# The value sums of the decode sequences in two accumulator banks by turns

## The chip, the cores and the metric

One core of one Trainium2 chip runs the whole program in one launch. The metric is the device time in microseconds (us). The kernel before takes 1522.09 us, the median of 3 runs (1521.27 to 1523.09).

## What is computed

One inference step of a decoder layer. 1024 prompt tokens go through a projection, causal differential attention (4 heads), a diagonal state-space mixer ("S5"), an output projection and a routed mixture of experts. Eight further sequences, of one new token each, go through the same layer, but their attention reads a paged cache of 8192 past positions: 64 pages of 128 positions for keys and as many for values, 256 KB a page and cache. For each of these sequences the reference has

```
s = einsum(q, k_all);  p = softmax(s)
a = p[:, :, 0] - lam * p[:, :, 1]
o = einsum('bhqk,bkhe->bqhe', a, v_all)
o = o * rsqrt(mean(o * o)) * subln_g * (1 - lambda_init)
```

The change is in the sums over `v_all` of these eight sequences.

## The kernel before, in words

**Passes.** The eight sequences are taken in two passes x of four (`SPP` = 4). A pass has a key part (units `K`), its softmax (`m1`, `m2`, `m3`, `pt`), and then the four sequences y = 0 to 3 of the value part, one after the other. The pages of a sequence come in eight steps `V(x, y, t, g)` of eight pages: t is the quarter (0 to 3), g the half of the ring of 16 page buffers that the step reads. Each step is two parts p of four pages. TensorE multiplies a page with a block of the transposed weights `sall` and adds into the PSUM bank `SC`, all eight steps of a sequence into the same sums; behind the last part stands one product for the new token (`dv`, `ptn`), which signals `s_pv`. Then comes `ov(b)`, b = 4x + y: VectorE copies the 128x512 sums to `o4s` (L1181), scales a small map (L1182) and signals `s_o4`; TensorE multiplies `o4s` with the map, four "closing" products into `aP`, four columns of the bank `OD`; VectorE copies these to `aD` (L1185). In the trace every matmul has the line L1756; a value step shows as SC<-ring,sall x16, the new token as SC<-dv,ptn, the closing products as OD<-wmap,o4s.

**Waits.** There is one bank for the sums, so the first step of the next sequence waits for the copy: `pe.wait_ge(s_o4, SPP * x + y)` (L1934). The pages are loaded by SyncE (L484); it waits before each four of them until TensorE is done with the buffers (`s_pgfree`). A TensorE step waits until its four pages are there (`landed`).

**The order.** Nothing is reordered at run time. `streams()` writes ten lists of units, each with an assumed cost and what it must come after; `make_plan()` (L177) merges them into one list, at each step the first list (`dec`, with K, V and ov) that is ready. Value steps become ready by assumed page landings and a fixed pace, so their place depends little on the other units. Every engine then runs its own share of each unit in this one order, and an engine that waits in one unit does nothing of a later one. Units on the way:

- prompt side: `q` projection and its rotation on VectorE, `qt`, and for each of 8 row blocks and 4 heads `S` (scores, VectorE takes the maximum), `C` (VectorE combines the two softmaxes), `T` (transposes), `O` (product with V), `AN` and `ot` per block;
- S5: `bA`, `bP`, `bK`, `bX`, `bH` (the scan, a long VectorE unit), `bY`, `bG`, `bS`, in four rounds;
- the end: `out` (output projection), `hn`, `hs`, `hT`, `r` (router), then the routing chain `pick1`, `pick2`, `rank`, `rt0`, `rt1`, `ids`, `lists`. `lists` (L1628, VectorE) has a part that needs nothing of `ids` and one that does, and ends in the signal `s_route` (L1663), for which the first expert weights (SyncE, L503) and the first gather of rows (GpSimd, L671) wait. `dout`, `dout2` and `out(8)` finish the eight sequences.

Around each change of sequence the order of the kernel before is:

- 0 to 1: V(0,0,3,1), bG(2,1), q(0,0), bS(2), bU(3), bA(3), q(0,1), V(0,1,0,0), ov(0), bP(3), V(0,1,0,1), qt(0)
- 1 to 2: C(0,3), bX, q(3,0), V(0,1,3,1), C(1,0), T(0,3), bH(3), q(3,1), V(0,2,0,0), ov(1), O(0,3), T(1,0), S(1,1), AN(0), V(0,2,0,1), C(1,1), ot(0)
- 2 to 3: V(0,2,3,1), O(2,1), S(2,2), V(0,3,0,0), ov(2), S(2,3)
- after 3: V(0,3,3,1), C(4,0), T(3,3), q(6,1), ov(3), O(3,3), K(1,0,0,0)
- 4 to 5: V(1,0,3,1), hs(2), out(3,1,0), hT(2), V(1,1,0,0), ov(4), r(2)
- 5 to 6: V(1,1,3,1), r(4), out(5,1,1), V(1,2,0,0), ov(5)
- 6 to 7: V(1,2,3,1), hn(7), hs(7), V(1,3,0,0), ov(6), hT(7), r(7), V(1,3,0,1), pick1
- after 7: rt1, V(1,3,3,0), ids, V(1,3,3,1), lists, ov(7), dout, dout2, out(8), turn0

Behind the plan stands the mixture of experts, a loop over experts whose weights (3 MB each) are loaded four ahead.

Of the kernel before, what the change touches and what calls it, by code (L numbers as in the profile page):

```python
# [6 lines left out]
SEQ, NB, D = 1024, 8, 1024  # L7
# [9 lines left out]
GRP = 8  # L17
TURNS = NPAGE // RING
SPP = 4
# [60 lines left out]
def streams():  # L80

    dec = []
    for x in range(NPASS):
        for t in range(TURNS):
            for g in range(2):
                for y in range(SPP):
                    dec.append((("K", x, t, g, y), 1.95, [(("ov", SPP * x - 1), 0.8)] if x else []))
        dec += [(("m1", x), 0.8, [(dec[-1][0], 0.9)]), (("m2", x), 0.3, [(("m1", x), 3.3)]),
                (("m3", x), 0.3, [(("m2", x), 1.0)]), (("pt", x), 2.3, [(("m3", x), 3.2)])]
        for y in range(SPP):  # L90
            b = SPP * x + y
            for t in range(TURNS):
                for g in range(2):
                    late = [(("pt", x), 1.2)] if t + g + y == 0 else [(dec[-2][0], 1.2)] if t + g == 0 else []
                    dec.append((("V", x, y, t, g), 1.95, late))
                    if t + g == 0 and y:
                        dec[-1], dec[-2] = dec[-2], dec[-1]
            dec.append((("ov", b), 0.4, [(("V", x, y, TURNS - 1, 1), 1.5)]))
    dec += [(("dout",), 0.1, [(("ov", NB - 1), 1.0)]), (("dout2",), 0.2, [(("dout",), 2.0)]),
            (("out", NT), 4.0, [(("dout2",), 1.0), (("out", NT - 1, 1, 1), 0.0)]), (("hn", NT), 0.0, [(("out", NT), 2.0)]),  # L100
            (("hs", NT), 0.0, [(("hn", NT), 2.5)]), (("hT", NT), 1.0, [(("hs", NT), 0.8)]),
# [146 lines left out]
def hymba_step(nc, io):  # L248
# [13 lines left out]
    with ctx:  # L262
# [122 lines left out]

        SC = ctx.enter_context(nc.psum_tensor("SC", [128, 512], f32))
        OD = ctx.enter_context(nc.psum_tensor("OD", [128, 512], f32))
        nkP, mxT, mbP, lP, aP = OD[0:32, 0:NB], OD[0:1, 128:256], OD[:, 256:257], OD[:, 257:258], OD[:, 260:264]
        WA = ctx.enter_context(nc.psum_tensor("WA", [128, 512 * BANKS], f32))
        W = [WA[:, 1024 * i:1024 * i + 1024] for i in range(3)]  # L390

# [580 lines left out]
        def _(dve):  # L972
# [196 lines left out]
            def pt(x):  # L1169
                dve.wait_ge(s_pexp, x + 1)  # L1170
                dve.tensor_tensor(mrow[:, 2:3], mrow[:, 2:3], mrow[:, 3:4], ADD)
                dve.drain().then_inc(s_l, 1)

            def ov(b):
                x, y = divmod(b, SPP)
                if y == 0:
                    dve.wait_ge(s_lP, x + 1)
                    dve.reciprocal(mrow[:, 4:5], lP)
                    dve.drain()
                dve.wait_ge(s_pv, b + 1)  # L1180
                dve.tensor_copy(o4s[:, :], SC[:, :])  # L1181
                dve.tensor_scalar(wmap[:, SPP, :], wmap[:, y, :], mrow[:, 4:5], None, MUL)  # L1182
                dve.drain().then_inc(s_o4, 1)  # L1183
                dve.wait_ge(s_aP, b + 1)
                dve.tensor_copy(aD[:, :, b], aP)  # L1185
                dve.drain().then_inc(s_ad, 1)

            def dout():
# [483 lines left out]
            def turn0():  # L1672
# [1 line left out]
                dve.drain().then_inc(free_sem("t0"), 1)  # L1674

            todo = {"stats": stats, "dqkv": dqkv, "dprep": dprep, "u": u, "k": k, "q": q, "S": S, "C": C, "O": O, "AN": AN,
                    "m1": m1, "m2": m2, "m3": m3, "pt": pt, "ov": ov, "dout": dout, "dout2": dout2, "s5a": s5a, "bA": bA, "bK": bK,
                    "bE": bE, "bH": bH, "bY": bY, "bG": bG, "glu": glu, "out": out_, "hn": hn, "hs": hs, "hT": hT,
                    "r": r_, "pick1": pick1, "pick2": pick2, "rt0": rt0, "rt1": rt1, "lists": lists, "turn0": turn0}
            for unit in PLAN:  # L1680
# [73 lines left out]
        def _(pe):  # L1754
# [163 lines left out]
            def pt(x):  # L1918
                pe.wait_ge(s_pexp, x + 1)
                for n in range(4):  # L1920
                    vacant(pe, "PT", x, n)
                    for j in range(4):
                        last = pe.transpose(slot("PT", x, n)[:, 128 * j:128 * j + 128],
                                            sall[:, n, 128 * j:128 * j + 128], ident)
                    last.then_inc(full_sem("PT", x, n), 1)
                vacant(pe, "PTn", x)
                pe.transpose(slot("PTn", x)[0:NB, 0:128], snew[:, :], ident).then_inc(full_sem("PTn", x), 1)
                pe.wait_ge(s_l, x + 1)
                mm(lP, consts[:, C_SUM:C_SUM + 128], mrow[:, 2:3]).then_inc(s_lP, 1)

            def Vv(x, y, r, g, p):
                if r + g + p == 0:
                    if y:
                        pe.wait_ge(s_o4, SPP * x + y)  # L1934
                    else:
                        pe.wait_ge(s_ptw, x + 1)
                landed(x, SPP * UPB + UPB * y + 2 * r + g, g, p)
                for j in range(p, GRP, PARTS):

                    t, q, c = j // 2, j % 2, j // 2  # L1940
                    blk = sall[:, r, 256 * g + 128 * q:256 * g + 128 * q + 128]
                    last = mm(SC[32 * c:32 * c + 32, :], blk[:, 32 * t:32 * t + 32], ring[:, GRP * g + j, :],
                              r + g + p == 0, r == TURNS - 1 and g == 1 and p == PARTS - 1 and c > 0,
                              skip_group_check=True)
                last.then_inc(s_pgfree, 1)
                if r == TURNS - 1 and g == 1 and p == PARTS - 1:
                    mm(SC[0:32, :], ptn[:, 0:32], dv[:, :], False, True, skip_group_check=True).then_inc(s_pv, 1)

            def ov(b):
                pe.wait_ge(s_o4, b + 1)  # L1950
                for h in range(H):
                    last = mm(aP[:, h:h + 1], o4s[:, 128 * h:128 * h + 128], wmap[:, SPP, h:h + 1])
                last.then_inc(s_aP, 1)

            def dout():
# [325 lines left out]
```

## Time and profile before

| what | value |
|---|---|
| median of 3 runs | 1522.09 us |
| the profiled execution | 1525.98 us |
| its span, first to last instruction | 1524.3 us |
| TensorE busy | 1307.3 us, 86% of the span |
| VectorE busy | 522.8 us, 34% |
| ScalarE, GpSimd busy | 247.9, 212.9 us |
| DMA | 458.35 MB, mean 301 GB/s |
| mean granted TensorE clock | 0.923 of full speed |

The page also has the span in 40 slices of 38 us. The first pass of value sums lies between 325 and 587 us, the second between 838 and 1069 us, the experts from about 1086 to 1470 us. In a timeline row the bracket at the end is the idle time of that engine before the row and what ended it. The granted clock has two levels, 1.0 (2.4 GHz) and 0.5 (1.2 GHz); a figure between is a mean over a stretch.

### The profile page before, as it was taken

Reading aid. Unit: us, or ns where it says so; the run is one execution under the profiler, and the core shown is the slowest. Engines: PE = TensorE matmul, PEld = TensorE weight load, DVE = VectorE, ACT = ScalarE, POOL = GpSimd, SP = SyncE. Lnnn points to the kernel's source line nnn. Section 1 sums busy time; section 2 is a strip of 40 time slices with the busy share of each in tenths; the row PEclk is TensorE's granted clock in tenths of the full one; section 3 lists DMA queues with packets and bytes.
Section 4 is the critical chain, followed back from the end, with each engine's and each line's share of the span. In section 5 each row is a group of like instructions: output and inputs, shape, how many; then the busy total and the mean of one; then the engine's idle time right before and its main releaser. Section 6 shows DMA issues by size and latency. Waiting matters only on the chain.

```text
span 1524.3 us, 26488 instructions
## 1 busy us (share of the span) xinstructions
PE 1307.3 (86%) x8952; PEld 686.1 (45%) x8952; DVE 522.8 (34%) x1430; ACT 247.9 (16%) x473; POOL 212.9 (14%) x327
## 2 busy tenths in 40 slices
PE   4899899999878877999877999986789999999930
PEld 2455565654424334666663434343344444444410
DVE  1452334443375354554431111134221211111227
ACT  2100111121112122332321000000011111111111
POOL 1102104041300200000010000000122222222111
PEclk9899999999898889999899999986899999999975
DMA  9499989889788976898897979897979999999854
GB/s 356 172 322 297 318 271 305 317 249 324 244 274 273 334 274 233 313 344 312 275 325 287 330 248 336 293 317 254 359 278 356 366 368 364 360 351 357 299 180 195
DMA packets 186454, 458.35 MB, mean 301 GB/s; under 512 B 24177, under 2 KB 24561, under 8 KB 177778
## 3 DMA queue, kind: packets, MB, share of 16 engines
q1 hardware_dynamic: 165906, 394.41, 73.6%
q0 software_dynamic: 20448, 62.59, 12.6%
q8 instruction: 66, 1.08, 0.3%
q14 instruction: 34, 0.28, 0.1%
HBM read 421.92 MB, written 33.80 MB: 299 GB/s over the span
## 4 chain that ended last, share of the span: by engine, by line
PE 67%; DMA 11%; DVE 9%; SPq 4%; issue 4%; DVEq 2%; ACT 1%; POOL 1%; ACTq 0%; POOLq 0%; PEldq 0%
PE WA L1756 48%; PE SC L1756 10%; PE OD L1756 4%; DMA ring<-in_cacheK 3%; DMA qpad<-h_scratch,idc 3%; SPq L484 2%; DMA ring<-in_cacheV 2%; PE WA L2098 2%; DMA arena<-in_x_s 1%; SPq L472 1%; DVE st L1100 1%; DMA ring<-h_scratch,idc 1%; PE WA L1857 1%; DVE arena L1725 1%; DVE arena L1738 1%
## 5 line engine op out<-in xcount | busy, mean ns | idle before, releaser
L1756 PE MATMUL WA<-arena 128*128 128x512 f32 (+10 forms) x1440 | 358.0, 436 | 26.2 <-issue 14.1
L1756 PE MATMUL WA<-arena,xm 128*128 128x512 f32 (+2 forms) x768 | 312.4, 610 | 7.6 <-DMA arena<-in_w_out 5.5
L1756 PEld LDWEIGHTS WA<-arena 128*128 128x128 f32 (+2 forms) x1440 | 196.7, 200 | 160.7 <-issue 138.3
L1756 PEld LDWEIGHTS WA<-arena,xm 128*128 128x128 f32 (+1 forms) x768 | 122.3, 179 | 160.7 <-issue 153.1
L1756 PE MATMUL SC<-ring,sall 128*32 128x512 f32 x1024 | 141.1, 671 | 35.8 <-DVEq L1183 21.9
L1756 PE MATMUL WA<-xm,arena 128*128 128x512 f32 x192 | 89.1, 612 | 1.7 <-ACT arena L931 1.3
L548 POOL TENSOR_TENSOR st<-st,consts 128x1 f32<-128x1 f32 (+2 forms) x18 | 13.8, 764 | 496.0 <-DVEq L1134 310.9
L1756 PEld LDWEIGHTS SC<-ring,sall 128*32 128x32 f32 x1024 | 28.0, 116 | 118.3 <-issue 66.6
L1756 PE MATMUL OD<-ring,qpad 128*32 128x128 f32 x2048 | 68.0, 286 | 10.5 <-DMA ring<-in_cacheK 10.4
L799 ACT ACTIVATE arena<-WA,st 128x128 f32<-128x128 f32 (+7 forms) x64 | 47.4, 741 | 146.5 <-DVEq L1104 146.5
L1756 PE MATMUL SC<-ring,qpad 128*32 128x128 f32 x2048 | 67.5, 286 | 3.8 <-DMA ring<-in_cacheK 3.8
L1756 PEld LDWEIGHTS OD<-ring,qpad 128*32 128x32 f32 x2048 | 57.1, 115 | 29.6 <-issue 16.9
L1668 DVE TENSOR_TENSOR xm<-WA,colw 128x960 f32<-128x960 f32 x16 | 18.5, 1158 | 147.9 <-PE WA L2098 147.9
L1756 PEld LDWEIGHTS SC<-ring,qpad 128*32 128x32 f32 x2048 | 57.3, 115 | 22.1 <-issue 16.5
L1668 DVE TENSOR_TENSOR arena<-WA,colw 128x960 f32<-128x960 f32 x16 | 18.5, 1158 | 140.4 <-PE WA L2098 140.2
L1756 PE MATMUL WA<-ring,xm 128*128 128x512 f32 x128 | 56.4, 593 | 0.0
L1756 PE MATMUL WA<-xm 128*128 128x512 f32 x128 | 56.3, 592 | 0.0
L666 POOL DMA_DIRECT2D y_dec<-arena x32 | 17.9, 558 | 273.3 <-ACT arena L938 273.3
L1756 PEld LDWEIGHTS WA<-xm,arena 128*128 128x128 f32 x192 | 35.9, 195 | 42.3 <-issue 40.7
L938 ACT ACTIVATE arena<-WA 128x1024 f32<-128x1024 f32 x32 | 32.8, 1024 | 131.2 <-PE WA L1756 131.2
L1100 DVE TENSOR_REDUCE st<-WA 128x1 f32<-128x128 f32 (+7 forms) x64 | 48.5, 758 | 5.3 <-issue 0.7
L1419 DVE TENSOR_TENSOR arena<-arena,WA 128x512 f32<-128x512 f32 x16 | 11.0, 688 | 111.6 <-PE WA L1756 86.4
(351 smaller groups left out, 1234.8 us busy)
## 6 DMA issues: line engine op xcount, KB each, us to landing
ring<-in_cacheK SPq DMA_DIRECT2D x512, 256.0 KB, 4.6
ring<-in_cacheV SPq DMA_DIRECT2D x512, 256.0 KB, 4.6
arena<-in_w_gu SPq DMA_DIRECT2D x16, 2048.0 KB, 10.0
arena<-in_w_dn SPq DMA_DIRECT2D x16, 1024.0 KB, 14.4
ring<-in_w_gu SPq DMA_DIRECT2D x8, 2048.0 KB
xm<-in_w_gu SPq DMA_DIRECT2D x8, 2048.0 KB, 10.4
arena<-in_w_in SPq DMA_DIRECT2D x32, 256.0 KB, 10.1
ring<-in_w_dn SPq DMA_DIRECT2D x8, 1024.0 KB
```

The costliest lines, as they stand in the source:

```text
L472: sp.dma_start(w[:, k, :], io["w_in"][n, k, :, :]).then_inc(s_wk[k], 16)
L484: sp.dma_start(ring[:, GRP * half + j, :], cache[bass.ds(pages[j], 1), :, :] .rearrange("a p n -> p (a n)")).then_inc(s_pg[PARTS * half + ...
L666: gp.dma_start(io["y_dec"][bass.ds(4 * NB * q + NB * v, NB), :], yb[v % 2][CAP:128, :]).then_inc(m_sd[v % 2], 16)
L799: act.activation(P[:, n % 2, c, 0:w], slot("S", i, h, c)[:, 0:w], ACT.Exp, bias=st[:, 4 * (n % 2) + c:4 * (n % 2) + c + 1], scale=HD ** -0 ...
L938: act.activation(yb[v % 2], W[1][:, :], ACT.Copy).then_inc(m_ys, 1)
L1100: dve.reduce_max(st[:, 8 + c:9 + c], S[:, 0:w], AX)
L1668: dve.tensor_tensor(hgT[v % 2][:, :, 0:CAP], (W[0] if src is None else src)[:, :] .rearrange("p (k n) -> p k n", k=KD)[:, :, 0:CAP], colw[ ...
L1725: dve.scalar_tensor_tensor(x1[0:r, i, :], yg[i][c][0:r, :], wts[0:r, c, i:i + 1], x1[0:r, i, :], MUL, ADD)
L1738: dve.scalar_tensor_tensor(x1[0:r, i, :], x1[0:r, i, :], st[0:r, i:i + 1], lnf[0:r, :], MUL, MUL)\
L1756: return pe.matmul(out, lhsT, rhs, start=first, stop=last, **kw)
L1857: last = pe.transpose(slot("AT", i, h)[:, 128 * j:128 * j + 128], P[:, n % 2, 0, 128 * j:128 * j + 128], ident)
L2098: last = pe.transpose((W[0] if out is None else out)[:, 128 * k:128 * k + CAP], hg[v % 2][0:CAP, 128 * k:128 * k + 128], ident[0:CAP, 0:CAP])
```

## The change

The sums of sequence y go into `SC` for even y and into `OD` for odd y. The first step of sequence y no longer waits for the copy of the sequence before; from y = 2 on it waits for the `aD` copy of the sequence two before (`s_ad`), for y = 1 that `lP` has been read (`s_l`). VectorE's copy of the sums to `o4s` moves out of `ov` into the last part of the sequence's last step, V(x, y, 3, 1), so it comes at that place in VectorE's order. The closing products go into four columns of the bank that was just copied, and `ov(b - 1)` stands behind V(x, y, 0, 1), one step later than before. `lP` and its reciprocal move into `pt`.

```
--- before
+++ after
@@ streams
-                    late = [(("pt", x), 1.2)] if t + g + y == 0 else [(dec[-2][0], 1.2)] if t + g == 0 else []
+                    late = [(("pt", x), 1.2)] if t + g + y == 0 else [(("ov", b - 2), 1.2)] if t + g == 0 and y >= 2 else []
                     dec.append((("V", x, y, t, g), 1.95, late))
-                    if t + g == 0 and y:
-                        dec[-1], dec[-2] = dec[-2], dec[-1]
-            dec.append((("ov", b), 0.4, [(("V", x, y, TURNS - 1, 1), 1.5)]))
+                    if y and t == 0 and g == 1:
+                        dec.append((("ov", b - 1), 0.5, [(("V", x, y - 1, TURNS - 1, 1), 2.5)]))
+        dec.append((("ov", b), 0.5, [(("V", x, y, TURNS - 1, 1), 2.5)]))
@@ VectorE
+                dve.wait_ge(s_lP, x + 1)
+                dve.reciprocal(mrow[:, 4:5], lP)
+                dve.drain().then_inc(s_l, 1)
+
+            def Vv(x, y, r, g, p):
+                if r < TURNS - 1 or g == 0 or p < PARTS - 1:
+                    return
+                dve.wait_ge(s_pv, SPP * x + y + 1)
+                dve.tensor_copy(o4s[:, :], (SC, OD)[y % 2][:, :])
                 dve.tensor_scalar(wmap[:, SPP, :], wmap[:, y, :], mrow[:, 4:5], None, MUL)
                 dve.drain().then_inc(s_o4, 1)
+
+            def ov(b):
                 dve.wait_ge(s_aP, b + 1)
-                dve.tensor_copy(aD[:, :, b], aP)
+                dve.tensor_copy(aD[:, :, b], (SC, OD)[b % 2][:, 260:264])
                 dve.drain().then_inc(s_ad, 1)
@@ TensorE
             def Vv(x, y, r, g, p):
+                acc = (SC, OD)[y % 2]
                 if r + g + p == 0:
-                    if y:
-                        pe.wait_ge(s_o4, SPP * x + y)
+                    if y == 0:
+                        pe.wait_ge(s_ptw, x + 1)
+                    elif y == 1:
+                        pe.wait_ge(s_l, 2 * x + 2)
                     else:
-                        pe.wait_ge(s_ptw, x + 1)
+                        pe.wait_ge(s_ad, SPP * x + y - 1)
...
             def ov(b):
                 pe.wait_ge(s_o4, b + 1)
                 for h in range(H):
-                    last = mm(aP[:, h:h + 1], o4s[:, 128 * h:128 * h + 128], wmap[:, SPP, h:h + 1])
+                    last = mm((SC, OD)[b % 2][:, 260 + h:261 + h], o4s[:, 128 * h:128 * h + 128], wmap[:, SPP, h:h + 1])
```

## Rows read from the trace of the kernel before

**Rows 1.** The page, part 1: busy time, share of the span, instructions.

```profile
PE 1307.3 (86%) x8952; PEld 686.1 (45%) x8952; DVE 522.8 (34%) x1430; ACT 247.9 (16%) x473; POOL 212.9 (14%) x327
```

**Rows 2.** The waits, whole span: us in total, times, longest.

```profile
DVE aD L1185 <- PE OD L1756: 32.1, 8, 6.6
...
PE SC L1756 <- DVEq L1183: 21.9, 6, 6.9
```

**Rows 3.** Timeline of TensorE, change 0 to 1: start, duration, engine, what.

```profile
376.25 1.04 PE L1756 MATMUL SC<-dv,ptn 8*32 8x512 f32 x2
...
388.63 3.64 PE L1756 MATMUL SC<-ring,sall 128*32 128x512 f32 x16 [4.28 <-DVEq L1183]
392.20 1.87 PE L1756 MATMUL OD<-wmap,o4s 128*128 128x1 f32 x8
...
395.81 3.64 PE L1756 MATMUL SC<-ring,sall 128*32 128x512 f32 x16
...
407.99 1.92 PE L1756 MATMUL SC<-ring,sall 128*32 128x512 f32 x16
```

**Rows 4.** Windows: length, busy PE, PEld, DVE, ACT, POOL; PEclk, DMA share, GB/s.

```profile
384.00:400.00 16.00, 11.72 (x52) 5.08 (x52) 4.16 (x13) 1.71 (x2) 5.29 (x11) 0.58 0.77 217
400.00:443.00 43.00, 39.42 (x240) 16.91 (x239) 25.29 (x85) 10.95 (x33) 4.21 (x8) 1.00 0.88 298
```

**Rows 5.** Timeline of VectorE, change 0 to 1.

```profile
376.00 0.72 DVE L1393 SCALAR_TENSOR_TENSOR arena<-arena,WA 128x544 f32<-128x544 f32 x1 [5.60 <-ACT arena L880]
...
387.62 0.69 DVE L1181 COPY o4s<-SC 128x512 f32<-128x512 f32 x1
```

**Rows 6.** Timeline of VectorE, change 1 to 2.

```profile
436.57 0.35 DVE L1116 SCALAR_TENSOR_TENSOR arena<-arena,st 128x128 f32<-128x128 f32 x1
...
452.27 0.69 DVE L1181 COPY o4s<-SC 128x512 f32<-128x512 f32 x1 [0.17 <-issue]
...
459.29 0.35 DVE L1126 TENSOR_SCALAR arena<-WA,st 128x128 f32<-128x128 f32 x1 [0.47 <-PE WA L1756]
```

**Rows 7.** Timeline of TensorE, change 1 to 2.

```profile
441.53 1.04 PE L1756 MATMUL SC<-dv,ptn 8*32 8x512 f32 x2
```

**Rows 8.** Timeline of TensorE, the later changes of sequence.

```profile
515.30 1.19 PE L1756 MATMUL SC<-ring,sall 128*32 128x512 f32 x8 [3.87 <-DVEq L1183]
518.01 1.93 PE L1756 MATMUL SC<-ring,sall 128*32 128x512 f32 x8 [1.51 <-DMA ring<-in_cacheV]
...
586.85 1.05 PE L1756 MATMUL OD<-wmap,o4s 128*128 128x1 f32 x8 [3.10 <-DVEq L1183]
...
894.89 3.59 PE L1756 MATMUL SC<-ring,sall 128*32 128x512 f32 x16 [2.64 <-DVEq L1183]
...
956.52 1.93 PE L1756 MATMUL SC<-ring,sall 128*32 128x512 f32 x16 [1.92 <-DVEq L1183]
...
1009.77 2.44 PE L1756 MATMUL SC<-ring,sall 128*32 128x512 f32 x16 [2.31 <-DVEq L1183]
```

**Rows 9.** Timeline of VectorE at the end of the routing chain.

```profile
1055.49 0.81 DVE L1635 TENSOR_TENSOR arena<-rt,consts 1x640 f32<-1x640 f32 x1 [0.25 <-issue]
...
1062.47 0.21 DVE L1651 SCALAR_TENSOR_TENSOR arena<-WA,arena 128x52 f32<-128x52 f32 x1 [4.21 <-PE WA L1756]
...
1064.00 0.17 DVE L1662 COPY idc<-ids 128x4 uint32<-128x4 uint32 x1
1066.91 0.69 DVE L1181 COPY o4s<-SC 128x512 f32<-128x512 f32 x1 [2.73 <-PE SC L1756]
...
1068.91 0.17 DVE L1185 COPY aD<-OD 128x4 f32<-128x4 f32 x1 [1.17 <-PE OD L1756]
```

**Rows 10.** Timeline of TensorE there: the products of ids.

```profile
1055.37 7.07 PE L1756 MATMUL WA<-arena 128*128 128x52 f32 x32 [3.64 <-DVEq L1625]
```

**Rows 11.** The chain that ended last: start, duration, what.

```profile
1083.97 24.12 DMA qpad<-h_scratch,idc
```

**Rows 12.** Windows, the start of the experts.

```profile
1068.00:1110.00 42.00, 28.91 (x161) 15.21 (x162) 8.52 (x22) 2.30 (x5) 4.77 (x6) 0.84 0.98 338
```

More of the change, by code:

```diff
@@ L387, in hymba_step @@
         OD = ctx.enter_context(nc.psum_tensor("OD", [128, 512], f32))
-        nkP, mxT, mbP, lP, aP = OD[0:32, 0:NB], OD[0:1, 128:256], OD[:, 256:257], OD[:, 257:258], OD[:, 260:264]
+        nkP, mxT, mbP, lP = OD[0:32, 0:NB], OD[0:1, 128:256], OD[:, 256:257], OD[:, 257:258]
         WA = ctx.enter_context(nc.psum_tensor("WA", [128, 512 * BANKS], f32))
@@ L1172, in pt @@
                 dve.drain().then_inc(s_l, 1)
[L1174 to L1181, printed above, removed]
+                dve.wait_ge(s_lP, x + 1)
[6 more added lines that the diff above has]
+                dve.tensor_copy(o4s[:, :], (SC, OD)[y % 2][:, :])
                 dve.tensor_scalar(wmap[:, SPP, :], wmap[:, y, :], mrow[:, 4:5], None, MUL)
                 dve.drain().then_inc(s_o4, 1)
+            def ov(b):
                 dve.wait_ge(s_aP, b + 1)
-                dve.tensor_copy(aD[:, :, b], aP)
+                dve.tensor_copy(aD[:, :, b], (SC, OD)[b % 2][:, 260:264])
                 dve.drain().then_inc(s_ad, 1)
@@ L1676, in _ @@
             todo = {"stats": stats, "dqkv": dqkv, "dprep": dprep, "u": u, "k": k, "q": q, "S": S, "C": C, "O": O, "AN": AN,
-                    "m1": m1, "m2": m2, "m3": m3, "pt": pt, "ov": ov, "dout": dout, "dout2": dout2, "s5a": s5a, "bA": bA, "bK": bK,
+                    "m1": m1, "m2": m2, "m3": m3, "pt": pt, "V": Vv, "ov": ov, "dout": dout, "dout2": dout2, "s5a": s5a, "bA": bA, "bK": bK,
                     "bE": bE, "bH": bH, "bY": bY, "bG": bG, "glu": glu, "out": out_, "hn": hn, "hs": hs, "hT": hT,
@@ L1925, in pt @@
                     last.then_inc(full_sem("PT", x, n), 1)
+                    if n == 0:
+                        pe.wait_ge(s_l, 2 * x + 1)
+                        mm(lP, consts[:, C_SUM:C_SUM + 128], mrow[:, 2:3]).then_inc(s_lP, 1)
                 vacant(pe, "PTn", x)
                 pe.transpose(slot("PTn", x)[0:NB, 0:128], snew[:, :], ident).then_inc(full_sem("PTn", x), 1)
-                pe.wait_ge(s_l, x + 1)
-                mm(lP, consts[:, C_SUM:C_SUM + 128], mrow[:, 2:3]).then_inc(s_lP, 1)
             def Vv(x, y, r, g, p):
+                acc = (SC, OD)[y % 2]
                 if r + g + p == 0:
-                    if y:
-                        pe.wait_ge(s_o4, SPP * x + y)
+                    if y == 0:
+                        pe.wait_ge(s_ptw, x + 1)
+                    elif y == 1:
+                        pe.wait_ge(s_l, 2 * x + 2)
                     else:
-                        pe.wait_ge(s_ptw, x + 1)
+                        pe.wait_ge(s_ad, SPP * x + y - 1)
                 landed(x, SPP * UPB + UPB * y + 2 * r + g, g, p)
@@ L1941, in Vv @@
                     blk = sall[:, r, 256 * g + 128 * q:256 * g + 128 * q + 128]
-                    last = mm(SC[32 * c:32 * c + 32, :], blk[:, 32 * t:32 * t + 32], ring[:, GRP * g + j, :],
+                    last = mm(acc[32 * c:32 * c + 32, :], blk[:, 32 * t:32 * t + 32], ring[:, GRP * g + j, :],
                               r + g + p == 0, r == TURNS - 1 and g == 1 and p == PARTS - 1 and c > 0,
@@ L1946, in Vv @@
                 if r == TURNS - 1 and g == 1 and p == PARTS - 1:
-                    mm(SC[0:32, :], ptn[:, 0:32], dv[:, :], False, True, skip_group_check=True).then_inc(s_pv, 1)
+                    mm(acc[0:32, :], ptn[:, 0:32], dv[:, :], False, True, skip_group_check=True).then_inc(s_pv, 1)
             def ov(b):
```

## The prediction, made before the change was run

> **What bounds the kernel now.** I read the page first, then the waits, then the timelines of TensorE and VectorE around each of the eight ends of a sequence, then the chain and the windows at the start of the experts. TensorE is busy 86% of the span and VectorE 34% [rows 1]: the end is set by TensorE and by what it waits for. In the waits the line of this change is L1183, the drain behind the copy to `o4s`: six first steps of a sequence waited 21.9 us for it [rows 2], and two closing products waited as well, one of them 3.10 us [rows 8]. VectorE stood 32.1 us in its eight waits for the closing products [rows 2].
>
> The stalls cost more than their own length. After the one of 4.28 us a value step of 16 matmuls took 3.64 us, again 3.64 us at 395.81, and only at 407.99 its usual 1.92 [rows 3]; the granted clock was 0.58 from 384 to 400 us and 1.00 after it [rows 4], so TensorE ran at 1.2 GHz before it came back to 2.4.
>
> DMA was busy 0.88 of the stretch behind it [rows 4]: TensorE can go faster there by about a tenth before pages are late.
>
> **The change part by part.** Each change of sequence is worked out from the order of before, since the value steps keep their places by the page pace and only `ov` moves behind the second step. The question each time: when is VectorE at the copy, and what is now behind that copy.
>
> *0 to 1.* TensorE had nothing to wait for at 384.35 (388.63 less 4.28) and all pages in place, since no page wait follows. Removed: the stall 4.28, two value steps at 3.64 instead of 1.92 (3.44), the closing products at 1.87 instead of the 1.05 that they take at full clock [rows 8] (0.8). That is 8.5 us. Added: VectorE waits at the copy until TensorE ends the sequence at 377.29 [rows 3] and copies, about 1.0 us with the drain, while before it started `bG` at 376.00 [rows 5]. So `bA` and the rotation of `q` end 2.3 us later, at about 389.5 instead of the 387.2 that lies before the copy [rows 5]. `qt` needs that rotation, and TensorE gets there at about 391: hidden. I take 7 of 8.5, since DMA has little left.
>
> *1 to 2.* Here the stall was the longest, 6.9 [rows 2], and the copy's new place hurts. Before, VectorE ended `C(0,3)` at 436.92 and worked 15.4 us without a stop (C(1,0), the scan bH(3), the rotation of q) to 452.27 [rows 6]; TensorE ended the sequence at 442.57 [rows 7]. After, the copy stands in front of that work: VectorE idles from 436.9 to 442.6, copies until 443.6, and ends the same 15.4 us at 459.0. Before, it went on with `O(0,3)` at 459.29 [rows 6], its wait for the closing products included. So `AN(0)` and `ot(0)` come 0.3 us earlier at most. TensorE runs ahead through two value steps and `ov(1)` and then stands at `ot(0)` for some 10 us, and comes back at 1.2 GHz. In the 12 us behind it lie one value step and more prompt work that ran at full clock; a value step alone loses 1.7 [rows 3]. From both sides: a gain of 1, or a loss of 6 if all of the work of such a stretch doubles (half of 12). I take a loss of 1.5, nearer to the row of the one step, since some of the slowed work lies beside VectorE's.
>
> *2 to 3.* The stall of 3.87 ended at 515.30, but the second half of the same step waited for pages until 518.01 [rows 8]. The pages end this step, not the copy. What is won is the closing products behind it at 1.2 GHz, moved off the path of S(2,3): 1.5. Bounds 0 and 3.9.
>
> *After 3.* `ov(3)` waited 3.10 [rows 8] because VectorE did the rotation of q first. The copy now stands ahead of it: 3.1. C(4,0) is behind the copy and up to 2 us later, hidden by q(6,1).
>
> *4 to 5 and 5 to 6.* VectorE has little to do and TensorE nearly never stands. Removed: 2.64 and a step at 3.59 instead of 1.93, then 1.92 [rows 8]: 6.2 us. `hs(2)` moves behind the copy but is needed only 3.6 us later, after `out`. I take 6; 3 if pages are late.
>
> *6 to 7.* 2.31 and 0.5 of clock [rows 8]. What follows at once is the routing chain, whose `hT(7)` waits now for `hs(7)`, which stands behind the copy. I take 2.3; 0 to 4.
>
> *The end, after 7.* This is a cost. Before, `lists` ran on VectorE when rt1 was done: from 1055.49, 2.8 us that need nothing of `ids`, beside the products of ids on TensorE, which lasted until 1062.4 [rows 10], then 1.7 us to 1064.2 [rows 9]. Only then did VectorE wait 2.73 for TensorE's last value step and copy at 1066.91. Now the last V stands ahead of `lists`: VectorE waits through `ids` and the last step, copies 1066.91 to 1067.8, and does both parts of `lists` after it, 2.8 + 1.8 = 4.6, to 1072.4. `s_route` comes 8.2 us later against the last value step. All expert weights and the first gather hang on it. DMA was busy 0.98 from 1068 to 1110 [rows 12], and the chain goes through a gather that took 24.12 us [rows 11] behind those weights: the first turns of the experts end with DMA, so the 8.2 us are paid in full. Bounds: 8.2, and 3.6 if only the `aD` copy, now behind `lists`, counts (1072.5 against 1068.91 [rows 9]). I take 8.2.
>
> *The rest.* The `lP` product and its reciprocal are moved into `pt`, two small instructions a pass (the nearest rows: 0.17 for a small copy [rows 9], 1.05 for four closing products [rows 8]) beside transposes; the copies and products are as many as before: nothing, within 1 us either way. The first step from y = 2 on waits for an `aD` copy made some 50 us earlier: nothing. The order can shift at near ties by the changed costs of `ov` (0.5 for 0.4); I give it 3 us either way.
>
> Sum: 7 - 1.5 + 1.5 + 3.1 + 6 + 2.3 - 8.2 = 10.2 us saved. Between the passes lie the keys and the prompt's attention, a fixed order in which a shift of TensorE and VectorE together is kept. The profiled execution took 1525.98 us with a span of 1524.3; it would be 1515.8. It stands 3.9 above the median of 1522.09, so the median becomes 1511.9.
>
> **A rule that says more.** VectorE began the first two copies 10.3 and 9.7 us after the sums were ready (387.62 against 377.29, 452.27 against 442.57), because it was at other work [rows 3, 5 to 7]; the one bank made TensorE wait for that. The Trainium skill ("Perfetto Trace Analysis", section Matmuls) has independent groups of matmuls rotate through different PSUM banks so that the evacuation of one overlaps the matmuls of the next. By it the whole wait goes; what it leaves out is where the evacuation stands in its own engine's order. That is the first rival.
>
> **The rivals.** *All stalls go.* If other VectorE work is not missed at 1 to 2 (the planner puts the scan ahead of the last value step, or TensorE finds enough to do), the saving is the 21.9 and 3.1 of stalls, and some 8 of clock, less 8.2: 25 us, 1497. For: TensorE has work in the order behind each stall. Against: the 15.4 us of VectorE work [rows 6] and the page wait at 518 [rows 8].
>
> *Given back.* VectorE, or the pages, become the bound in the first pass: then only 3.1 + 6 + 2.3 remain against 8.2, a saving of 3, 1519. For: the 0.88 of DMA [rows 4]; VectorE's wait is only moved.
>
> *Slower: the early copy holds up VectorE.* One mechanism, an engine that waits in its order for a copy that nobody needs yet. At the end it costs 8.2 for sure if the order stays; at 1 to 2 up to 6. It decides when the first pass saves less than 0: 8.2 + 6 - 7 - 3.1 and half of the second pass's 8.3 lost to pages gives +0, and with the stall of 0 to 1 also given back +7: 1529. For: `lists` behind the copy [rows 9] follows from the order itself. Against: five of eight places have nothing of weight behind the copy.
>
> **How the numbers follow.** Forecast 0.46, all stalls go 0.17, given back 0.18, slower 0.19. The time is that of the forecast, 1512. The range runs from 1499 to 1526: it takes in most of the first rival, the whole of the second and a part of the third. What a measurement of this kernel can tell from no change is 0.2%, 3.0 us. Faster: the forecast nearly whole (0.44), the first rival (0.17) and a third of the second (0.06), 0.67. Same: the rest of the second and slips of the others, 0.15. Slower: 0.18.
>
> **What would show it.** In the profile after, the wait of SC or OD for the drain behind the copy should be gone but for the last `ov`; the first step of sequence 1 should take 1.9 us at full clock, and TensorE should stand long once behind `ov(1)`, for VectorE. VectorE should have a new wait before L1181's copy of some 6 us at 1 to 2 and of some 10 us at the end. From the last SC or OD<-dv,ptn to the indirect gather there should be about 6 us, where before the gather started ahead of it. It is wrong if `lists` is done before the last copy, or if the gather on the chain does not move with `s_route`.

## The result and the profile after

| | before | after |
|---|---|---|
| median of 4 runs | 1522.59 us (1521.27 to 1528.69) | 1481.95 us (1480.03 to 1488.01) |
| ratio, 95% interval | | 0.9732 [0.9693, 0.9772] |
| profiled execution, span | 1525.98, 1524.3 us | 1488.01, 1486.3 us |
| granted TensorE clock | 0.923 | 0.938 |

The change made the kernel 40.6 us faster. The forecast was 1512, with a range down to 1499: the sign was right and the size four times too small. Timed twice more beside other kernels, the changed kernel gave 0.9767 [0.9706, 0.9827] and 0.9739 [0.9687, 0.9791]. One kernel's runs spread by up to 26 us (16 of the changed kernel: 1472.9 to 1492.8, mean 1482.5; 76 of the kernel before, its one slow run left out: 1509.0 to 1534.8, mean 1520.4), so below I use means over all series of a kernel. A figure behind ± is half the 95% interval of a difference of means, worked out from the single runs.

The page of the changed kernel, part 1, beside [rows 1]: TensorE has 24 us less to do at the same number of instructions; the mean clock of 0.938 for 0.923 accounts for about 21 of them (1307.3 times 1 - 0.923/0.938, an estimate).

```profile
PE 1282.9 (86%) x8952; PEld 671.4 (45%) x8952; DVE 522.2 (35%) x1430; ACT 247.8 (17%) x473; POOL 212.8 (14%) x327
```

The waits of TensorE in the changed kernel (us in total, times, longest). The 21.9 us behind the copy of [rows 2] have no successor. Beside a wait for ScalarE that was there before (20.1 us, now 21.8), pages and the softmax combination (L1118, 9.9 before) lead now.

```profile
PE OD L1759 <- DMA ring<-in_cacheK: 17.4, 5, 6.7
PE WA L1860 <- DVEq L1118: 17.0, 9, 5.6
PE OD L1759 <- DMA ring<-in_cacheV: 12.1, 9, 2.9
PE WA L1878 <- DVEq L1140: 10.7, 4, 4.2
```

Timeline of TensorE in the changed kernel: the first step of sequence 1, where [rows 3] had 3.64 us and a stall of 4.28, and the closing products of sequence 7, the only ones that still wait for a copy.

```profile
385.64 1.92 PE L1759 MATMUL OD<-ring,sall 128*32 128x512 f32 x16
...
401.58 1.94 PE L1759 MATMUL OD<-ring,sall 128*32 128x512 f32 x8 [2.93 <-DMA ring<-in_cacheV]
...
1032.76 1.05 PE L1759 MATMUL OD<-wmap,o4s 128*128 128x1 f32 x8 [0.95 <-DVEq L1184]
```

Windows of the changed kernel, columns as in [rows 4]. From 384 to 400 the clock is 1.00 for 0.58 and DMA is full (1.01 for 0.77); behind it TensorE waits for pages (2.93 us at 401.58, above) and the clock is lower than before (0.84 for 1.00). In this profile the change 0 to 1 gained next to nothing, though its stall is gone.

```profile
384.00:400.00 16.00, 14.66 (x108) 7.16 (x107) 7.47 (x20) 3.33 (x4) 9.65 (x19) 1.00 1.01 258
400.00:443.00 43.00, 36.10 (x182) 14.02 (x183) 23.55 (x71) 8.06 (x26) 3.44 (x7) 0.84 0.88 290
```

Timeline of VectorE in the changed kernel at 1 to 2 and at the end, beside [rows 6] and [rows 9]. At 1 to 2 the copy has no idle time in front of it: the scan was done first (the sums were ready at 443.81, the copy came 7.9 us later, and TensorE did not wait for it). At the end `lists` (L1638 to L1665) is over before the copy, which the prediction had behind it.

```profile
451.74 0.69 DVE L1182 COPY o4s<-OD 128x512 f32<-128x512 f32 x1
...
1018.59 0.81 DVE L1638 TENSOR_TENSOR arena<-rt,consts 1x640 f32<-1x640 f32 x1 [0.25 <-issue]
...
1027.11 0.17 DVE L1665 COPY idc<-ids 128x4 uint32<-128x4 uint32 x1
1031.85 0.69 DVE L1182 COPY o4s<-OD 128x512 f32<-128x512 f32 x1 [4.57 <-PE OD L1759]
1033.85 0.17 DVE L1188 COPY aD<-OD 128x4 f32<-128x4 f32 x1 [1.17 <-PE OD L1759]
```

The reason is the planner. The new place of `ov` in the stream "dec" moved about 80 of its 523 units. In the first pass bK(3), bE(3), the bX(3), the scan bH(3) and bY(3) come earlier; near the end r, pick1, rank, ids come earlier, and `lists` stands ahead of V(1,3,3,1). So two things had been changed at once, the mechanism (banks, place of the copy) and the order, and the experiments take them apart.

Time between the ends of the value sums (starts of `<-dv,ptn`), one profile each, us:

| kernel | first end | 0-1 | 1-2 | 2-3 | 3-4 | 4-5 | 5-6 | 6-7 | last to span's end | span |
|---|---|---|---|---|---|---|---|---|---|---|
| before | 376.3 | 65.3 | 67.2 | 70.0 | 308.0 | 61.4 | 58.3 | 59.4 | 458.5 | 1524.3 |
| after | 377.6 | 65.2 | 65.1 | 61.4 | 300.2 | 55.4 | 56.2 | 49.8 | 455.5 | 1486.3 |
| after, second profile | 372.5 | 60.3 | 68.1 | 60.4 | 299.9 | 55.4 | 57.9 | 50.0 | 456.6 | 1481.1 |
| after, third | 373.1 | 61.4 | 64.9 | 58.7 | 300.8 | 55.4 | 56.2 | 50.2 | 458.6 | 1479.2 |
| e2, banks alone | 374.8 | 57.0 | 67.9 | 66.5 | 302.4 | 55.4 | 56.3 | 55.1 | 458.7 | 1494.0 |
| e18, the same | 375.8 | 56.7 | 68.3 | 66.6 | 301.7 | 55.4 | 58.0 | 54.2 | 459.2 | 1495.8 |
| e1, order alone | 377.0 | 65.0 | 70.6 | 66.3 | 303.5 | 63.0 | 58.2 | 53.8 | 455.0 | 1512.5 |
| e13, e2 with the scan ahead | 372.9 | 56.8 | 60.6 | 64.5 | 301.2 | 55.4 | 58.0 | 54.7 | 458.8 | 1482.8 |
| e12, the changed kernel with the scan behind | 376.0 | 59.7 | 71.4 | 59.6 | 300.9 | 55.4 | 56.2 | 52.4 | 455.2 | 1486.8 |
| e16, the same | 371.3 | 60.7 | 77.6 | 59.9 | 296.9 | 55.4 | 56.2 | 50.1 | 460.8 | 1488.9 |
| e3, lists last | 374.9 | 61.3 | 64.7 | 59.5 | 297.5 | 55.4 | 56.2 | 52.2 | 464.2 | 1485.9 |

Profiles of one kernel show what such a row can tell: 4-5 repeats to 0.1 us, the stretches of the first pass only to 3 to 6 us, and from the last sum to the end e12 and e16 differ by 5.6.

### The profile page after: what moved, and what is told of

The parts are those of the page before. It is cut to its first block, busy times and chain, and to the rows that moved or that the text cites. A ratio compares the mean times of both kernels' runs of the same rounds, so it can differ in the third digit from the quotient of the medians.

```text
span 1486.3 us, 26489 instructions
## 1 busy us (share of the span) xinstructions
PE 1282.9 (86%) x8952; PEld 671.4 (45%) x8952; DVE 522.2 (35%) x1430; ACT 247.8 (17%) x473; POOL 212.8 (14%) x327
## 4 chain that ended last, share of the span: by engine, by line
PE 70%; DMA 9%; DVE 8%; SPq 6%; issue 3%; DVEq 2%; ACT 1%; POOL 0%; ACTq 0%; POOLq 0%; PEldq 0%
PE WA L1759 52%; PE SC L1759 7%; PE OD L1759 6%; DMA ring<-in_cacheK 5%; SPq L484 4%; DMA ring<-in_cacheV 2%; PE WA L2105 2%; SPq L472 1%; DVE st L1100 1%; PE WA L1860 1%; DVE arena L1728 1%; DMA ring<-h_scratch,idc 1%; DVE arena L1741 1%; DMA xm<-in_xT 1%; PE WA L2065 1%
## 5 line engine op out<-in xcount | busy, mean ns | idle before, releaser
L1759 PE MATMUL WA<-arena 128*128 128x512 f32 (+9 forms) x1440 | 351.1, 428 | 21.6 <-issue 10.2
L1759 PEld LDWEIGHTS WA<-arena 128*128 128x128 f32 (+2 forms) x1440 | 192.4, 195 | 155.4 <-issue 139.3
L1759 PE MATMUL OD<-ring,qpad 128*32 128x128 f32 x2048 | 66.8, 283 | 17.4 <-DMA ring<-in_cacheK 17.4
L1759 PE MATMUL OD<-ring,sall 128*32 128x512 f32 x512 | 70.0, 660 | 12.1 <-DMA ring<-in_cacheV 12.1
L1759 PE MATMUL SC<-ring,qpad 128*32 128x128 f32 x2048 | 66.5, 282 | 6.1 <-DMA ring<-in_cacheK 5.8
L1759 PE MATMUL SC<-ring,sall 128*32 128x512 f32 x512 | 63.5, 616 | 1.8 <-DMA ring<-in_cacheV 1.8
L1759 PE MATMUL WA<-xm 128*128 128x512 f32 x128 | 56.3, 592 | 0.0
## 6 DMA issues: line engine op xcount, KB each, us to landing
arena<-in_w_dn SPq DMA_DIRECT2D x16, 1024.0 KB, 12.3
ring<-in_w_dn SPq DMA_DIRECT2D x8, 1024.0 KB, 12.5
```

Of the source, the lines that this page charges most:

```text
L1759: return pe.matmul(out, lhsT, rhs, start=first, stop=last, **kw)
```

## The experiments

All were timed beside the kernel before on the same chip; "interval" is the 95% interval of the ratio. "Old order" is the planner's order of the kernel before, "new order" that of the changed one. The last column says which of the theories written down before each run, printed below, the time bore out.

| run | banks | order | median us | ratio | interval | bore out |
|---|---|---|---|---|---|---|
| e1 | one | new | 1515.24 | 0.9954 | [0.9922, 0.9986] | A |
| e8 | one | old, new behind K(1,3,0,0) | 1516.79 | 0.9973 | [0.9948, 0.9998] | between A and B |
| e11 | one | new, old behind K(1,3,0,0) | 1523.71 | 1.0032 | [0.9999, 1.0066] | I, above its range |
| e2 | two | old | 1498.61 | 0.9857 | [0.9813, 0.9902] | none, between 1497 and 1512 |
| e18 | two | old (e2 again) | 1500.43 | 0.9872 | [0.9825, 0.9918] | O |
| e4 | two, copy late | old | 1499.71 | 0.9853 | [0.9807, 0.9899] | B |
| e7 | two, copy of sequence 1 late | old | 1502.79 | 0.9895 | [0.9866, 0.9925] | neither, 3 us above both |
| e5 | two | old, new behind K(1,3,0,0) | 1496.04 | 0.9844 | [0.9799, 0.9889] | B |
| e6 | two | new, old behind K(1,3,0,0) | 1489.16 | 0.9802 | [0.9768, 0.9835] | between, nearer B |
| e13 | two | old, scan ahead | 1491.68 | 0.9825 | [0.9774, 0.9877] | N |
| e14 | two | old, scan and lists ahead | 1487.81 | 0.9801 | [0.9755, 0.9846] | N2 missed by 2 us |
| e12 | two | new, scan behind | 1496.50 | 0.9855 | [0.9803, 0.9907] | N, above its range |
| e16 | two | e12 again | 1489.43 | 0.9811 | [0.9764, 0.9858] | between W and N |
| e3 | two | new, lists last | 1492.69 | 0.9812 | [0.9769, 0.9855] | A |
| e10 | two, copy late | new | 1494.46 | 0.9824 | [0.9772, 0.9876] | P, above its range |
| e15 | two | a third order | 1495.25 | 0.9826 | [0.9776, 0.9877] | L |
| e9 | two | new (the changed kernel) | 1483.00 | 0.9767 | [0.9706, 0.9827] | as expected |
| e17 | two | new (the changed kernel) | 1479.82 | 0.9739 | [0.9687, 0.9791] | O |

### Banks or order

e1 is the kernel before with the new order, e2 the changed kernel with the old one; both set `ov` by hand, e1 behind the first step of the next sequence, e2 behind the second:

```
+    for b in range(NB):
+        x, y = divmod(b, SPP)
+        if y < SPP - 1:
+            plan.remove(("ov", b))
+            plan.insert(plan.index(("V", x, y + 1, 0, 1)) + 1, ("ov", b))   # e1: 0, 0
```

> The kernel before (one bank, the copy in ov, the wait for it in front of the next sequence) with the order of units that the planner makes for the changed kernel; only ov is put back behind V(x, y+1, 0, 0), where one bank needs it. Theory A (the banks do it): the seven waits for the copy are still there, some 22 us and the slow clock behind them, so it saves at most 8 us, 1515 to 1523. Theory B (the planner's new order does it, my prediction took the order as unchanged): it saves 20 us or more, 1480 to 1502. Theory C (both, about half each): 1500 to 1512.

> The changed kernel with the order of units of the kernel before; only ov stands behind V(x, y+1, 0, 1). This is the kernel that my prediction worked out: 1512, with the copy 5.7 us ahead of the scan at the change 1 to 2 (VectorE idle from the end of C(0,3)), and s_route 8 us later against the last value step. If the rule of rotating banks holds whole and the early copy costs nothing: 1490 to 1497. If the early copy takes all back: 1520 to 1529.

> The changed kernel again, beside e18 on one chip. Theory O (the order is worth 13 to 16 us with two banks): 1480 to 1486. Theory B (banks are nearly all of it, and the rest was a difference between series): 1486 to 1494, less than 8 us below e18.

> Two banks and the early copy in the order of the kernel before, again. Theory O: 1496 to 1501. Theory B: 1490 to 1496.

> The changed kernel once more, on the chip of the three below, so that they have a base. Both theories: 1482 us (1480 to 1490), 0.973 of the kernel before. It also says how far the segments between the ends of the sequences vary for one and the same code: by what the kernels with equal order showed, 0.1 us in the second pass, up to 4 us in the first.

e2 is the kernel that the prediction had worked out. Over 12 runs it stands at 1499.9, 20.4 us (± 2.5) below the mean before. The changed kernel stands 17.4 (± 3.6) lower still (1482.5), and 20.6 by the medians on one chip (e17 against e18). The order alone, with one bank, gave 7 us (± 4.4), and the waits for the copy are still there in its profile (19.3 us in six places). So the two are not independent: 20.4 and 7 make 27, together they give 38.

e2 at 1 to 2, TensorE and under it VectorE. The prediction had the copy wait 5.7 us for TensorE, and TensorE stand "some 10 us" at `ot(0)` (L1889):

```profile
431.72 1.04 PE L1770 MATMUL OD<-dv,ptn 8*32 8x512 f32 x2
...
441.52 1.05 PE L1770 MATMUL OD<-wmap,o4s 128*128 128x1 f32 x8
...
453.23 1.11 PE L1889 MATMUL WA<-consts,arena 128*128 128x128 f32 x4 [10.66 <-DVEq L1151]
```

```profile
432.80 0.69 DVE L1193 COPY o4s<-OD 128x512 f32<-128x512 f32 x1 [5.70 <-PE OD L1770]
```

### The place of the copy

e4 leaves the copy in `ov`, which then stands behind the second step; e7 does so for sequence 1 alone; e10 is e4 in the new order.

```
-            def Vv(x, y, r, g, p):
-
-                if r < TURNS - 1 or g == 0 or p < PARTS - 1:
-                    return
-                dve.wait_ge(s_pv, SPP * x + y + 1)
+            def ov(b):
+                y = b % SPP
                 dve.wait_ge(s_pv, b + 1)
                 dve.tensor_copy(o4s[:, :], (SC, OD)[y % 2][:, :])
```

> Two banks in the order of before as in e2, but the copy to o4s stays in ov and so comes behind V(x, y+1, 0, 1) in VectorE's order. Theory A (the early copy holds VectorE up at the change 1 to 2 and at the end): 8 us at the end and 1 to 6 at the scan less than e2, so 9 to 14 us below it, about 1500. Theory B (an early copy is harmless, a late one delays ov on TensorE): equal to e2 or up to 8 us above it.

> e2 with one copy moved: that of sequence 1 stands in ov again, behind the scan bH(3) in VectorE's order; the other seven stay early. Theory A (VectorE idles 5.7 us in front of the scan, as my prediction had it): the stretch from the end of sequence 1 to that of sequence 2 falls from 67.9 by about 5, and the time by 2 to 5, 1493 to 1497. Theory B (the scan is not missed): no change, 1497 to 1500.

> The changed kernel with its own order, but the copy of the sums in ov, behind the second step of the next sequence. Theory M (the second bank alone is the mechanism, the place of the copy decides nothing): within 4 us of the changed kernel, 1482, as it was in the old order (1498.6 with the copy early, 1499.7 with it late). Theory P (the early place is worth something once the scan lies ahead of it, since the last steps then find o4s filled): 1487 to 1492. In both the closing products wait again for the copy where VectorE is busy.

In the old order the place is worth nothing that the runs can tell (e4 against e2: 0.9 ± 4.6 us). It exchanges one wait for others: the 10.66 of `ot(0)` goes, and in e4 the closing products wait:

```profile
446.52 1.87 PE L1766 MATMUL OD<-wmap,o4s 128*128 128x1 f32 x8 [6.51 <-DVEq L1193]
...
567.94 1.50 PE L1766 MATMUL OD<-wmap,o4s 128*128 128x1 f32 x8 [3.10 <-DVEq L1193]
```

e7 shortened 1-2 by 3.1 us (64.8 against 67.9) and lost 4.2 in 2-3 (70.7 against 66.5): the local mechanism was right, the gain was not kept, and the time rose rather than fell (3.9 ± 4.5 us above e2). Its profile is of a run of 1510.2, 7 us above the median of its series, so it says little of the rest. In the new order the early place was worth 11 us (e10 1494.5 against e9 1483.0, same chip; 9.8 ± 7.8 by means). Its closing products wait 3.10, 1.65 and 0.38 us for the copy, 5.1 us that the changed kernel doesn't have. Between the two profiles lie 3.7 us in 1-2 (71.8 against 68.1) and 6.0 in 3-4 (305.9 against 299.9); what the 6 us there are is open.

### Which part of the order

e5, e6, e8 and e11 join the two orders at K(1,3,0,0) in the second pass, a point up to which both have placed the same 383 units.

```
+    one, two = make_plan(), make_plan(streams_other())    # the planner on either kernel's streams
+    cut = 383
+    one, two = one[:cut], two[cut:]
...
+    return one + two
```

> Two banks and the early copy. Units up to K(1,3,0,0) stand in the order of the kernel before, all behind it in the order of the changed kernel. There the new order differs only from sequence 6 on: r(6), hT(7), r(7) and pick1 are ahead of value steps that they stood behind, and lists is ahead of the last one. Theory A (the rest of the gain behind e2's comes from the end of the order): 10 us or more below e2, 1482 to 1489. Theory B (it comes from the first pass, where most units moved): equal to e2, 1496 to 1502.

> The reverse of e5: two banks and the early copy, the new order up to K(1,3,0,0), the order of before behind it. Theory A: near e2, 1494 to 1502. Theory B: near the changed kernel, 1480 to 1487.

> The kernel before, one bank, with the new order from K(1,3,0,0) on and ov behind V(x, y+1, 0, 0). Theory A (the new end is worth the same without the second bank): 5 to 10 us below before, about 1514, the same as e1. Theory B (it needs the second bank): within 3 us of before.

> One bank and the copy of the kernel before; the new order in the first pass, the old one from the first keys of the second pass on. Theory I (the reorder and the second bank need each other: with one bank the earlier scan only shifts where VectorE is late for the copy): 1515 to 1521, less than 5 us saved. Theory S (the order of the first pass is worth the same 8 us with either mechanism): 1511 to 1514. The stall at 1 to 2 should be shorter in both, since the scan lies ahead of it: 3 us or less against 6.9 before.

With two banks the means are 1499.9 (old), 1495.0 (new end), 1488.4 (new first pass), 1482.5 (both): 4.9 (± 8.5) and 11.5 (± 5.6) against 17.4 together. With one bank the new first pass gave nothing (e11, ratio 1.0032). Its waits for the copy say why; they were 21.9 us in six places [rows 2]:

```profile
PE SC L1866 <- DVEq L1293: 19.2, 6, 5.0
```

All six are still there. The scan ahead shortened the one at 1 to 2, as expected, from 6.92 to 3.10 us, but the one at 2 to 3 grew from 3.87 to 4.98. With two banks none of them is left; at 1 to 2 of e2 TensorE stands instead for something else that is queued behind the copy, and that is what an order can mend. This is my reading of why the two parts need each other; the numbers behind it are e11's and e13's below.

e13, e14 and e12 (with e16) move single units:

```
+    plan.remove(("bH", 3))
+    plan.insert(plan.index(("V", 0, 1, 3, 1)), ("bH", 3))         # e13, e14; e12 and e16: index + 1
+    plan.remove(("lists",))
+    plan.insert(plan.index(("V", 1, 3, 3, 1)), ("lists",))        # e14; e3: index + 1
```

> Two banks and the early copy in the order of the kernel before (e2, 1498.6), with one unit moved: the scan bH(3) just ahead of the last value step of sequence 1. Theory N (that near tie alone carries the gain of the order in the first pass): 1487 to 1492, as the whole new first-pass order gave (1489.2). Theory W (the gain needs the rest of the order too): 1495 to 1500, within 4 us of e2.

> The changed kernel with one unit moved: the scan bH(3) goes back behind the last value step of sequence 1, so the copy stands in front of it, as the prediction had assumed. Theory N (this one near tie is what the order brought in the first pass, the condition of the prediction's first rival): 1 to 2 and 2 to 3 together take 5 us and more longer and the median is 1488 to 1492. Theory W (the gain of the order is spread over many units, none of them decisive): within 3 us of the changed kernel.

> The kernel with the scan behind the last value step of sequence 1 and everything else as in the changed kernel, once more. Theory N: 1492 to 1498 again, and a profile of a run near that median shows where the time stands. Theory W: 1481 to 1486, the first series was chance.

The scan put ahead of the last value step, and nothing else, takes e2 from 1499.9 to 1491.2 (mean of 6; 8.7 ± 7.4); put back behind it in the changed kernel, it takes that from 1482.5 to 1493.1 (mean of 12; 10.6 ± 4.3; the two series, 1496.5 and 1489.4, lie apart by more than I had allowed). So this one unit is worth 9 to 11 us by the means (6 and 13 by the ratios to the kernel before), about half of the order's part. The profiles say the same: from the first end to the fourth, the three stretches of the first pass, e2 and e18 took 191.4 and 191.6 us, e13 and e14 with the scan ahead 181.8 and 182.2. In e13 the stall at `ot(0)` is all but gone, with a wait of 3.08 for the softmax combination ahead of it; TensorE, then the windows of e2 and of e13:

```profile
439.72 0.44 PE L1873 MATMUL WA<-consts,arena 128*128 128x128 f32 x2 [3.08 <-DVEq L1131]
...
445.70 0.66 PE L1891 MATMUL WA<-consts,arena 128*128 128x128 f32 x4 [0.44 <-DVEq L1153]
```

```profile
443.00:510.00 67.00, 46.55 (x250) 22.46 (x250) 34.25 (x114) 15.66 (x43) 13.01 (x22) 0.79 0.75 261
```

```profile
443.00:510.00 67.00, 57.49 (x317) 26.92 (x310) 32.22 (x104) 18.12 (x49) 11.22 (x20) 0.92 0.90 311
```

TensorE gets 11 us more of busy time into the same 67 (8.4 more from 384 us on), at a clock of 0.92 for 0.79, and DMA rises with it: the wait, the clock behind it and the idle queue come together. 1-2 took 60.6 us for 67.9. In the changed kernel TensorE waits 5.61 us for the softmax combination at 1 to 2, in e12 and e16 8.53 and 8.52, and 1-2 takes 64.9 to 68.1 in the one and 71.4 and 77.6 in the others.

> The changed kernel with value steps planned at 2.0 us instead of 1.95: the planner then gives a third order, with 74 of the units at other places than in the changed kernel and 84 at others than in the kernel before, but with the scan ahead of the last value step of sequence 1 and lists ahead of the last value step, as in the changed kernel. Theory N2 (the two ties decide): 1480 to 1487. Theory L (orders differ by luck in many small ways): anywhere from 1475 to 1500, most likely near 1492.

e15 has the scan and `lists` at the good side, and 74 other units elsewhere; it ran at 1495.25 (one of its six runs took 6042.53 us, is no time of the kernel and is left out of the ratio; the other five have a mean of 1493.8). So the two ties are not all of it: 11.3 us (± 5.8) hang on the rest. Its 2-3 took 71.2 us where the changed kernel took 58.7 to 61.4, with this wait for pages among others:

```profile
PE OD L1759 <- DMA ring<-in_cacheV: 4.1, 1, 4.1
```

Which units make that difference was not run down.

### The end

> As the one above, with lists also ahead of the last value step of the last sequence. Theory N2 (the two ties carry the whole gain of the order): 1480 to 1486, as the changed kernel. By the prediction's price of the end (8.2 us) it should stand 8 us below e13; by the third-turn reading of the profiles (the price was 2.6 in the old order, since the gather of the first turn was late by that much only) 2 to 3 us below it.

> The changed kernel with one unit moved: lists behind the last value step instead of ahead of it, as the order of before had it. Theory A (the price of the end that I predicted is real, the new order only avoids it): the gather starts about 10 us later against the rest, the first turns of the experts with it, and the time is 8 to 10 us above the changed kernel: 1489 to 1493. Theory B (hidden behind out(8) and turn0): within 3 us of it, 1479 to 1485.

e14, with `lists` ahead as well, has a mean of 1488.8, 2.4 us below e13 where the prediction's price would give 8.2; with ± 7.7 the runs alone can't tell the two apart. It also stands 6.3 (± 4.7) above the changed kernel: the two ties together don't bring the whole order.

e2 has at its end what the prediction said. VectorE, then GpSimd's gather:

```profile
1036.40 0.69 DVE L1193 COPY o4s<-OD 128x512 f32<-128x512 f32 x1 [11.65 <-PE OD L1770]
...
1041.85 0.17 DVE L1199 COPY aD<-OD 128x4 f32<-128x4 f32 x1
```

```profile
1042.10 1.06 POOL L671 DMA_INDIRECT qpad<-h_scratch,idc  x1 [57.29 <-DVEq L1677]
```

The gather starts 6.8 us behind the last sum (1035.32), before it started 1.3 ahead of it: 8.1 us later, as forecast. But from there to the end of the span e2 took 458.7 us and the kernel before 458.5. Other profiles with the same end agree in the main: 460.0 with one bank (e11), 459.2, 458.8, 458.6 and, once, 465.9 with two (e18, e13, e6, e7); the means are 459.2 with one bank and, e2 included, 460.2 with two. So the end cost about 1 us, with a scatter of single profiles that is much larger. The chain of waits of e2 goes through that first gather, which took half of the 24.12 of [rows 11]:

```profile
1042.10 12.16 DMA qpad<-h_scratch,idc
```

What counted before was the third gather, issued at 1083.97, 18.1 us behind the last sum; it hangs on the last token block (`hn(8)`, behind the `aD` copy), not on `lists`. GpSimd of the kernel before has the root of `hn(8)` and then, in its order, the second and this third gather:

```profile
1081.25 0.54 POOL L548 TENSOR_TENSOR st<-st,consts 128x1 f32<-128x1 f32 x1 [10.64 <-DVEq L1433]
1081.99 1.05 POOL L660 DMA_INDIRECT ring<-h_scratch,idc  x1 [0.20 <-issue]
...
1083.97 1.01 POOL L660 DMA_INDIRECT qpad<-h_scratch,idc  x1 [0.30 <-issue]
```

In e2 the third gather is issued at 1057.00, 21.7 behind the last sum: 3.5 later, about the prediction's lower bound of 3.6, and even that doesn't show in the time to the end.

The same move in the new order was not free: e3 stands 10 us above the changed kernel (1492.2 against 1482.5 in means, ± 4.2), and from last sum to end it took 464.2 us for the 455.5 to 458.6 of the changed kernel's three profiles; one profile alone wouldn't carry that (e7 above). Its chain holds both gathers, the third issued 25.9 us behind the last sum (1021.68) and as slow as before; in the changed kernel it is 19.6 behind (1050.41 against 1030.77):

```profile
1028.45 12.39 DMA qpad<-h_scratch,idc
...
1047.59 23.01 DMA qpad<-h_scratch,idc
```

In the new order turn0 stands ahead of `hn(8)`; so the late `lists` holds up the first gather, that holds up turn0 on TensorE and VectorE, and `hn(8)` and the third gather come behind. In the old order `hn(8)` stands ahead of turn0. So there is a price of about the predicted size, but in an order that the prediction did not look at and by another path.

None of the kernels beat the changed one; e14 (1487.8) came nearest.

## Why the prediction was wrong, step by step

Its own kernel is e2, and against that its terms can be read one by one (mean of the two profiles of e2, e2 and e18, against the one of the kernel before; saved, us). The profile before is of a run 5.5 us above its kernel's mean, those of e2 lie 3.3 below theirs, so the measured terms add up to some 9 us too much, and it is not known in which of them that lies:

| term | predicted | measured | |
|---|---|---|---|
| 0 to 1 | 7 | 8.4 | right: clock 1.00 for 0.58, no wait; DMA gave nearly all of the 8.5 |
| 1 to 2 | -1.5 | -0.9 | right, with both waits (5.70, 10.66) |
| 2 to 3 | 1.5 | 3.4 | within its bounds |
| after 3, to 4 | 3.1 | 5.9 | 3.1 of stall, and 3 within what 3-4 varies (300.9 and 296.9 in e12 and e16, one kernel) |
| 4 to 5, 5 to 6 | 6 | 7.1 | right in sum: 55.4 and 57.2 for 61.4 and 58.3, more at the first than its 4.3, less at the second than its 1.9 |
| 6 to 7 | 2.3 | 4.7 | above its bound of 4; what the rest is was not run down |
| the end | -8.2 | -0.5 | wrong (-1.0 over all profiles with this end) |
| sum | 10.2 | 28 (1.0 more ahead of the first end) | by the runs 20.4 |

**The step that failed** is the first sentence of the working: "Each change of sequence is worked out from the order of before, since the value steps keep their places by the page pace and only `ov` moves". Replayed, the planner shifts the value steps too, by at most 4.7 us of its own time; but the prompt's units around them changed places (the scan comes 10 us earlier), and 17.4 of the 38 us came from the new order. The sum had "The order can shift at near ties by the changed costs of `ov` (0.5 for 0.4); I give it 3 us either way". It was not the 0.1: with 0.4 put back in the changed kernel's planner, two units move, and put alone into the planner before, the new cost, delay or condition each move one unit or none. It was the new place of `ov` in the stream: it no longer stands ahead of the second value step, something else is planned there, and from there near tie after near tie falls the other way.

**The term that was mis-sized** is the end: "the first turns of the experts end with DMA, so the 8.2 us are paid in full". The delay of the first gather came as worked out (8.1 us), the payment did not (about 1 us of 8.2). The gather of 24.12 us on the chain was taken for one that hangs on `lists`; it was the third, which hangs on `hn(8)`. The bound of 3.6, "if only the `aD` copy, now behind `lists`, counts", was the truth about the delay of the third gather. That is also the prediction's own sign of being wrong, "if the gather on the chain does not move with `s_route`". Without this term the sum would have been 18.4 us, and e2 gave 20.4.

**The other steps.** The first rival, all stalls go, 1497, named the right condition, "the planner puts the scan ahead of the last value step", and e13 shows that it decides some 9 us. It kept the 8.2 of the end; without it, it would have given 1489. *Given back* fell as a whole: the first pass saved 11 us in e2 and 10.8 to 17.5 in the changed kernel's profiles (184.9 to 191.6 us for 202.4). But in part it was right: at 0 to 1 e2 kept 8.4 us, while the changed kernel's profiles took 60.3 to 65.2 us for 65.3, with waits for pages. *Slower* fell: no two-bank kernel was slower than before. The signs named beforehand were right: no waits of the first steps, 1.92 us at full clock, and for e2 the waits at 1 to 2 and at the end; "wrong if `lists` is done before the last copy" is what the changed kernel shows. That the changed kernel came out faster, as forecast, owes nearly half of its size to an order that the prediction did not foresee: the sign was worked out, that part was luck.

The rule of the Trainium skill ("Perfetto Trace Analysis", section Matmuls), that groups of matmuls rotate through banks so that evacuation overlaps them, held for the accumulator's own wait: it is gone in e2 as in the changed kernel. What the prediction set against it, the place of the evacuation in its engine's order, is what e13 measured at some 9 us.

## What to carry to other kernels

Where a planner orders the work, replay it with the change before pricing anything: an edit that moved one kind of unit (`ov`) in a stream moved eighty others, and here that was nearly half of the gain. Here a second accumulator bank removed the wait for the copy of the sums, and then the order on the copying engine decided: work that TensorE needs soon (here the scan and what follows) belongs ahead of a copy that waits. And before a delay is charged in full to a long transfer on the chain, check which unit that very transfer waits for.

## What the runs showed of the hardware

- One kernel's runs spread by 26 us (before, 1509.0 to 1534.8), though parts of it repeat to 0.1 us: 4-5 took 55.4 or 55.5 us in every two-bank profile, while 0-1 of the changed kernel took 60.3 to 65.2. Two series of six runs of one kernel had medians 7 us apart (e12, e16), so here a smaller difference between two such series says nothing.
- The first gather of the experts took 12.2 to 12.5 us (e2, e18, e3), the third, of as many rows, 21.4 to 24.1 (before, e9, e17, e3); the second took 12.3 in the changed kernel's first profile. Which transfers beside it make the difference was not tested.
- DMA's mean busy share was 1.00 for 43 us while TensorE stayed at full clock: e2 from 400 to 443 us, clock 1.00, 337 GB/s for 298 before [rows 4], TensorE busy 38.05 us for 39.42; 0-1 took 57.0 us there for 65.3. A share of 1.01 or 1.02, as in other windows, shows that the figure is good to some hundredths only.
